# Products of the 64x64 inverse in four array tiles, with the second head's base written across the partition halves

## What is computed

```python
def wkv7_scan(r, w, k, v, kk, a, reverse):
    ...
    def step(state, inp):
        r_t, w_t, k_t, v_t, kk_t, a_t = inp
        sa = jnp.einsum('bhij,bhj->bhi', state, -kk_t)
        state = (state * w_t[:, :, None, :] + sa[..., None] * (kk_t * a_t)[:, :, None, :]
                 + v_t[..., None] * k_t[:, :, None, :])
        return state, jnp.einsum('bhij,bhj->bhi', state, r_t)
    ...
y = direction(0, False) + direction(1, True)
```

## Time and profile before

| | us |
|---|---|
| median of three runs | 3975.27 |
| lowest, highest | 3974.74, 3975.91 |
| the profiled execution | 3977.9 |
| its span, first to last instruction | 3976.1 |
| recurrence, layer 0 and layer 1 | 249.1 and 246.9 |

### The profile page before, as it was taken

How to read it: one execution, slowest core, us unless ns; L and a number is a source line. 1 busy time by engine, 2 the same in 40 slices (tenths; PEclk the granted TensorE clock), 3 DMA queues, 4 the chain that set the end, 5 groups by cost and what they waited for, 6 DMA issues and landing times.

```text
span 3976.1 us, 67100 instructions
## 1 busy us (share of the span) xinstructions
PE 3783.7 (95%) x28976; PEld 3059.2 (77%) x28976; DVE 1684.3 (42%) x2714; ACT 1439.1 (36%) x2442; POOL 1388.7 (35%) x581
## 2 busy tenths in 40 slices
PE   8888999999999889999999989999999999999999
PEld 7777778788887776688888776777888777787887
DVE  5554541577145554603682257414111376332112
ACT  3354252232323442523223243634222436424222
POOL 4001324434442002244444354133444443244443
PEclk9999999999999999999999999999999999999999
DMA  3001222276220002122473221112222221122222
GB/s 143 2 4 45 82 75 85 85 251 222 93 87 33 4 4 91 66 85 106 161 269 123 93 85 64 43 64 101 92 99 88 103 85 39 51 103 84 86 101 90
DMA packets 37150, 356.65 MB, mean 90 GB/s; under 512 B 4224, under 2 KB 4352, under 8 KB 17920
## 3 DMA queue, kind: packets, MB, share of 16 engines
q1 hardware_dynamic: 19584, 278.93, 18.9%
q10 hardware_dynamic: 17280, 73.48, 5.2%
HBM read 350.29 MB, written 2.10 MB: 89 GB/s over the span
## 4 chain that ended last, share of the span: by engine, by line
PE 84%; DVE 8%; ACT 3%; issue 2%; POOL 1%; DMA 1%; DVEq 0%; SPq 0%; PEldq 0%; ACTq 0%; PEld 0%; POOLq 0%
PE banks L757 23%; PE banks L759 23%; PE banks L758 22%; PE banks L1110 10%; PE banks L2151 3%; ACT arena L1471 1%; ACT arena L2304 1%; PE banks L2233 1%; POOL ring_r L855 1%; DMA ring<-stream 1%; DVE arena L1949 1%; DVE arena L2628 1%; PE banks L1217 0%; DVE arena L2627 0%; DVE arena L1843 0%
## 5 line engine op out<-in xcount | busy, mean ns | idle before, releaser
L855 POOL TENSOR_TENSOR ring_r<-ring,hi_ring 128x1024 fp32r<-128x1024 f32 x490 | 1202.4, 2458 | 2252.0 <-ACT hi_ring L846 2250.9
L757 PE MATMUL banks<-xT_r,ring_r 128*128 128x512 f32 (+1 forms) x2480 | 955.6, 385 | 25.8 <-issue 14.1
L759 PE MATMUL banks<-xT_r,hi_ring 128*128 128x512 f32 x2096 | 829.2, 396 | 0.0
L758 PE MATMUL banks<-x_lo_r,hi_ring 128*128 128x512 f32 x2096 | 825.4, 394 | 0.0
L846 ACT ACTIVATE hi_ring<-ring 128x1024 fp32r<-128x1024 f32 x490 | 511.3, 1047 | 734.0 <-DMA ring<-stream 289.2
L757 PEld LDWEIGHTS banks<-xT_r,ring_r 128*128 128x128 f32 x2480 | 472.5, 191 | 124.5 <-issue 26.7
L759 PEld LDWEIGHTS banks<-xT_r,hi_ring 128*128 128x128 f32 x2096 | 396.1, 189 | 94.1
L758 PEld LDWEIGHTS banks<-x_lo_r,hi_ring 128*128 128x128 f32 x2096 | 398.2, 190 | 90.3 <-issue 3.3
L1110 PE MATMUL banks<-arena 64*64 64x64 f32 (+4 forms) x7456 | 350.0, 246 | 53.0 <-DVE arena L1843 23.8
L1471 ACT ACTIVATE arena<-banks 128x512 f32<-128x512 f32 x366 | 214.7, 595 | 413.8 <-PE banks L759 255.2
L757 PE MATMUL banks<-hi_ring,pairs 128*128 128x512 f32 x864 | 341.8, 396 | 4.0 <-POOL ring_r L855 4.0
(11 more groups left out here) (263 smaller groups left out, 5504.1 us busy)
## 6 DMA issues: line engine op xcount, KB each, us to landing
ring<-stream SPq DMA_DIRECT2D x132, 2048.0 KB, 7.7
arena<-ada ACTq DMA_DIRECT2D x96, 512.0 KB, 4.9
arena<-ln_rows ACTq DMA_DIRECT2D x5, 1024.0 KB, 7.7
arena<-edge ACTq DMA_DIRECT2D x4, 1024.0 KB, 5.1
arena<-edge ACTq DMA_DIRECT2D x2, 1792.0 KB, 8.3
arena<-pack ACTq DMA_DIRECT2D x2, 1485.0 KB, 6.6
arena<-pack ACTq DMA_DIRECT2D x2, 1200.5 KB, 5.5
x<-x_in SPq DMA_DIRECT2D x4, 512.0 KB, 7.4
```

The lines of the kernel that those rows point to most:

```text
L757: first = nc.tensor.matmul(out_, left[1], right[0], start=start, stop=False)
L758: low = nc.tensor.matmul(out_, left[0], right[1], start=False, stop=False)
L759: return first, low, nc.tensor.matmul(out_, left[0], right[0], start=False, stop=stop)
L855: nc.gpsimd.tensor_tensor(feed.raw(n, ring_r), feed.raw(n), feed.hi(n).bitcast(F32), ALU.subtract).then_inc(split_lo, 1)
```

## The change

The operands keep their places except for head 1's part of `XT`, which now lies in the other partition half from the beginning. VectorE writes the base so: head 0 in one operation of 128 partitions, head 1 in two of 64 partitions, each into the opposite half. With this, x0, r0, inv_a and inv_x of all levels and wu run in four tiles, and inv_t of all levels in two, in bank 6. turned 0 becomes a product with the identity, in four tiles, that writes across the group's own two banks; it waits for gram 1's masks. turned 1 moves to bank 6. r0 moves from the beat of inv_a 4 to the beat of turned 2, into the group's own banks. wu's outputs are divided between its banks by head and no longer by chunk pair, so both banks are full at its end.

```diff
@@ -164,12 +164,12 @@
     b0, b1 = ((0, 1), (2, 3))[d]
     turned = [("v_rows", j, (6,))] if d == 0 else []
     out = [[("prep", g, (b0, b1))], [], [("prep_w", g, ())], [], [("prep_a", g, ())], [], [("prep_b", g, ()), ("prep_ar", g, ())],
-           [("gram", g, 0, (b0, b1))], [("gram", g, 1, (b0, b1)), ("unit", g, ())], [("turned", g, 0, (6,))] + turned,
-           [("x0", g, (b0,)), ("turned", g, 1, (b1,))], [("turned", g, 2, (6,))]]
+           [("gram", g, 0, (b0, b1))], [("gram", g, 1, (b0, b1)), ("unit", g, ())], [("turned", g, 0, (b0,))] + turned,
+           [("x0", g, (b0,)), ("turned", g, 1, (6,))], [("turned", g, 2, (6,)), ("r0", g, (b0,))]]
     for n in range(len(LEVELS)):
         last = n == len(LEVELS) - 1
-        banks_a, banks_x, banks_t = (b0,), (b0,) if n else (6,), (b0,) if n == 0 or last else (6,)
-        out += [[("inv_a", g, n, banks_a)] + ([("r0", g, (6,))] if last else []),
+        banks_a, banks_x, banks_t = (b0,), (b0,), (6,)
+        out += [[("inv_a", g, n, banks_a)],
                 ([] if last else [("inv_x", g, n, banks_x)]) + [("inv_t", g, n, banks_t)]]
     out += [[("wu", g, (b0, b1))], [("mq", g, (b0, b1))], [("oo", g, ())]]
     out += [[("link", g, i, (4 + i % 2,) if i < NC - 1 else ())] for i in range(NC)]
...
-        return name == "inv_t" and level in (0, len(LEVELS) - 1) or name in ("inv_a", "inv_x") and level > 0
+        return name in ("inv_a", "inv_x", "x0", "r0")
...
                 g, which = args
                 b = banks[0]
                 take(b, use[0])
-                for q in range(4):
-                    src = ARI[g % 3][:, 0, q * P:(q + 1) * P] if which == 0 else BB[g % 2][:, which - 1, q * P:(q + 1) * P]
-                    ins = nc.tensor.transpose(bank[b][:, q * P:(q + 1) * P], src, C("ident"))
+                if which == 0:
+                    drained(pe, uses, "gram", g, 1)
+                    for q in range(4):
+                        for e in range(2):
+                            for p_ in range(2):
+                                at = (4 * e + q) * CH
+                                ins = mm(across(b)[side(p_ ^ e), at:at + CH], ARI[g % 3][side(e), 0, (2 * q + p_) * CH:(2 * q + p_ + 1) * CH],
+                                         C("ident2")[side(e)], True, True)
+                else:
+                    drained(pe, uses, "turned", g, 0)
+                    for q in range(4):
+                        ins = nc.tensor.transpose(bank[b][:, q * P:(q + 1) * P], BB[g % 2][:, which - 1, q * P:(q + 1) * P], C("ident"))
                 ins.then_inc(bank_full[b], 1)
...
                 elif name == "r0":
                     drained(pe, uses, "gram", g, 1)
                     drained(pe, uses, "v_rows", g // 2)
+                    drained(pe, uses, "turned", g, 1)
                 elif name != "inv_a":
                     drained(pe, uses, "inv_a", g, args[1])
...
                             n, straight, crossed = 2 * q + e, side(p_), side(p_ ^ e)
-                            h = crossed if level and name in ("inv_x", "inv_t") else straight
-                            to = crossed if name == "inv_a" and level or name == "inv_t" and level < len(LEVELS) - 1 else straight
+                            h = straight if name in ("inv_a", "r0") else crossed
+                            to = straight if name in ("x0", "inv_x") else crossed
...
                 for q in range(4):
                     for e in range(2):
                         for p_ in range(2):
-                            h = side(p_)
-                            ins = mm(bank[banks[q // 2]][h, (q % 2 * 2 + e) * P:(q % 2 * 2 + e + 1) * P], XT[d][h, 2 * q + e, :],
+                            h = side(p_ ^ e)
+                            ins = mm(bank[banks[e]][side(p_), q * P:(q + 1) * P], XT[d][h, 2 * q + e, :],
                                      AR0[d][h, q, e, :, :].rearrange("p a t -> p (a t)"), True, True)
-                    if q % 2:
-                        ins.then_inc(bank_full[banks[q // 2]], 1)
+                        if q == 3:
+                            ins.then_inc(bank_full[banks[e]], 1)
...
-                out_ = AR0[d][:, :, :, 0, :] if which == 0 else GM[d][:, :, :, which - 1, 2, :]
-                f(out_, bank[b][:, :].rearrange("p (q e k) -> p q e k", q=4, e=2), ACT.Copy).then_inc(bank_free[b], 1)
-            elif name in ("inv_x", "inv_t") and wide(name, args[1]):
+                if which == 0:
+                    f(AR0[d][:, :, :, 0, :].rearrange("p q e k -> p e q k"), across(b).rearrange("p (e q k) -> p e q k", e=2, q=4), ACT.Copy)\
+                        .then_inc(bank_free[b], 1)
+                else:
+                    f(GM[d][:, :, :, which - 1, 2, :], bank[b][:, :].rearrange("p (q e k) -> p q e k", q=4, e=2), ACT.Copy)\
+                        .then_inc(bank_free[b], 1)
+            elif name in ("x0", "inv_x"):
...
                   across(b).rearrange("p (e q t) -> p e q t", e=2, q=4), ACT.Copy).then_inc(bank_free[b], 1)
-            elif name in ("x0", "inv_x", "inv_t"):
+            elif name == "inv_t":
...
-                f(AR0[args[0] % 2][:, :, :, 1, :], bank[b][:, :].rearrange("p (q e k) -> p q e k", q=4, e=2), ACT.Copy)\
+                f(AR0[args[0] % 2][:, :, :, 1, :].rearrange("p q e k -> p e q k"), across(b).rearrange("p (e q k) -> p e q k", e=2, q=4), ACT.Copy)\
                     .then_inc(bank_free[b], 1)
...
-                    f(WU[args[0] % 2][:, 2 * i:2 * i + 2, :, :, :].rearrange("p q e a t -> p (q e a t)"), bank[banks[i]][:, :], ACT.Copy)\
+                    f(WU[args[0] % 2][:, :, i, :, :].rearrange("p q a t -> p q (a t)"), bank[banks[i]][:, :].rearrange("p (q c) -> p q c", q=4), ACT.Copy)\
                         .then_inc(bank_free[banks[i]], 1)
...
                 low_t = GM[d][:, :, :, 0, 0, :].rearrange("p q e t -> p (q e) t")
                 up = C("first_L")[:, 64 * (1 - d):64 * (2 - d)]
                 link(V.tensor_tensor(low_t, low_t, C("ident2").unsqueeze(1).to_broadcast([P, 8, CH]), ALU.add))
-                V.tensor_tensor(XT[d], low_t, up.unsqueeze(1).to_broadcast([P, 8, CH]), ALU.mult).then_inc(first_done, 1)
+                by_head = [a.rearrange("p (q e) t -> p q e t", e=2) for a in (XT[d], low_t)]
+                V.tensor_tensor(by_head[0][:, :, 0, :], by_head[1][:, :, 0, :], up.unsqueeze(1).to_broadcast([P, 4, CH]), ALU.mult)
+                for h in range(2):
+                    ins = V.tensor_tensor(by_head[0][64 - 64 * h:128 - 64 * h, :, 1, :], by_head[1][64 * h:64 * h + 64, :, 1, :],
+                                          up[64 * h:64 * h + 64].unsqueeze(1).to_broadcast([CH, 4, CH]), ALU.mult)
+                ins.then_inc(first_done, 1)
```

## The result

The changed kernel takes **3998.62 us** (3990.03 to 4007.35, seven runs) where the kernel before, on the same chip, takes 3975.91 (3974.74 to 3983.31, seven runs): a ratio of 1.0052, 95% interval 1.0040 to 1.0063. It is slower by 0.5%, by 22.7 us. The forecast was 3962, its range ended at 3971, and slower had a chance of 0.05. The profiled execution took 4000.89 with a span of 3999.1, 23.0 more than before.

What follows compares the result with a forecast made beforehand. TensorE, busy in 95% of the span, was taken as the bound. Three even periods at 1.31 us, four odd at 0.69 and the ends gave 6.7 us a layer, 13.3 in two: 3975.3 became 3962 us, range 3951 to 3971.

Steps and rivals of the forecast that it cites:

- The pace of the products: TensorE in the recurrence: four tiles instead of two save 0.41 us per narrow product and 0.86 for wu.
- oo's pace: Feared for turned 0's 16 matmuls changing row halves: 1.05 us per 32 records against 0.51, costing 3 us in all.
- The base: VectorE before x0: three operations take 1.27 us instead of 0.69, 0.58 later, hidden under wu in even groups.
- The walk of a period: TensorE from gram 1 to oo in one group: gain of 0.44 us in even groups, loss of 0.18 in odd.
- From oo to the next gram 0: Later part of every period: inv_a 0 saves 0.41 us, and inv_a 1 starts 0.46 earlier through its new bank.
- The middle: Seven periods a layer between the ends: three even ones save 1.31 us each, four odd ones 0.69 each.
- Ends: First and last group of a layer: -1.0 against 0.87 us at the head, about +0.1 at the tail.
- rival (3): Added waits in the recurrence drop the clock to 1.2 GHz, two stretches per period, 45 us lost, 4007; chance 0.04.
- r0: Moved behind turned 2, where TensorE doesn't wait, it costs 0.51 us before oo in each group.
- (1): Rival: the recurrence's new waits are absorbed and nearly the bare sum of 26.9 us is saved, 3951; chance 0.10.
- (2): Rival: new waits eat more, each half-wide base operation taking 0.69 us, 3973; turned 0 possibly slow too; chance 0.18.
- (4): Rival: the recurrence's products stay at the two-tile pace because pairs meet in a bank, 3991; chance 0.02.

Runs made afterwards that it cites:

- a_base1: Changed kernel with VectorE's base as one 128x512 operation again (output not the reference's): 3998.6 us, ratio 1.0059.
- b_sh128: Kernel before with 32 tiny matmuls (128 TensorE instructions) added in the wait at the program's start: 3983.7 us, ratio 1.0007.
- a_fill: Changed kernel with products nobody reads in TensorE's waits, 32 at the head and 16 at the tail of each recurrence: 3985.6 us, ratio 1.0028.
- c_r0_head: Changed kernel with r0 at its old place in two tiles, output right, and products nobody reads at each head: 3968.4 us, ratio 0.9976.
- b_r0: Kernel before with r0 alone moved to the beat of turned 2, in two tiles as before: 3991.1 us, ratio 1.0043.
- a_r0old: Changed kernel with r0 back behind inv_a of level 4, in two tiles (output not the reference's): 3976.7 us, ratio 0.9999.
- a_sh64: Changed kernel with 16 tiny matmuls (64 TensorE instructions) added in the wait at the program's start: 3995.7 us, ratio 1.0037.
- c_r0: Changed kernel with r0 at its old place in two tiles, output right through two more ScalarE copies: 3974.5 us, ratio 0.9991.
- b_fill: Kernel before with products nobody reads in TensorE's waits at the head and tail of each recurrence: 3981.3 us, ratio 1.0021.
- a_w2: Changed kernel with eight products nobody reads in group 0 of each layer, before turned 0 and x0: 3983.3 us, ratio 1.0015.

## Why the prediction was wrong

**The pace of the products: right.** x0, r0, inv_a 0 and turned 0 at 0.69 to 0.73, wu at 1.10, as forecast from the earlier trace rows. turned 0 did not run at oo's pace.

**The base: its length right, its price too high.** Three operations from 278.71 to 280.00, 1.29 end to end where I took 1.27; VectorE's rows:

```profile
277.99 0.69 DVE L1849 TENSOR_TENSOR ring<-ring,const 128x512 f32<-128x512 f32 x1
278.71 0.42 DVE L1851 TENSOR_TENSOR arena<-ring,const 128x256 f32<-128x256 f32 x1
279.15 0.85 DVE L1853 TENSOR_TENSOR arena<-ring,const 64x256 f32<-64x256 f32 x2
```

0.42 + 0.85 and 0.02 between them: no overlap, where operations on the same partitions overlap by 0.09. The rule of the Trainium skill ("VectorE: DVE Perf Modes", section "Two Vector instructions with no wait between them") says that the crossing ones are held; the trace agrees. Against a_base1 the longer base delays x0 by 0.59 in the odd group, as forecast, but only 0.21 of it is left at the next gram 0, where my sum let all of it through.

**The walk of a period: misses that cancel, which is luck.** I let turned 0 and x0 start 0.1 before the last VectorE operation ends; they start 0.15 after it (280.00 to 280.15). So turned 0 comes at 5.17 after gram 0 and not at 4.94, and oo at 11.00 and 10.71 where the walk gave 10.62 and 10.44. So oo is 0.06 earlier in the even group and 0.45 later in the odd one, against 0.44 earlier and 0.18 later. From oo to the next gram 0 the forecast gave 0.87 and the trace gives 1.26 and 1.05. The sums, 1.32 and 0.60 a period against 1.31 and 0.69, agree only because of both.

**The middle: right without the stops.** Mean of after, its repeats and its shifts, against before and b_sh128: 437.2 - 24.4 = 412.8 against 434.3 - 10.8 = 423.5, 10.7 us less where the forecast's seven periods gave 13.4. (The few stops in heads and tails are taken off here too.)

**First failed step: a term that was not there.** The sum has no place for instruction supply. The stops grew by 13.6 us (24.4 against 10.8) and took the middle's gain. That they are waits for the instruction packet rests on the constant rest modulo 256 under two shifts, on one packet for every 256 instructions, and on the 2.15 us before which no boundary was crossed. Before, 4.4 us of "issue" stood among the waits of the same stretch; I did not ask what would make them more. The Trainium skill ("Runtime: NRT & Kernel Launch", section "Instruction fetch mechanics") says that the stream comes in blocks of 256 instructions and that crossing a boundary is mostly hidden. The block size agrees with the trace; hidden the crossing is here only where TensorE arrives 2.2 to 2.9 us after the packet's start or later. Four dense four-tile products are 256 instructions in about 2.05 us (a step of 0.51 each), four of two tiles take 3.7 (0.92 each): that is an estimate of why the shorter products stop and the longer ones seldom did. turned 0 adds 56 instructions a group.

**Second failed step: "Ends".** I put -1.0 + 0.87 on the head and +0.1 on the tail. At a clock of 1.00 the head of a_fill is 15.6 against 14.4 before, 1.2 longer where I had 0.13, so the head's term was mis-sized by about 1.1 a layer even without the clock (with r0 at its old place, c_r0_head, the head is 14.6). The clock came on top: 41.7 against 30.3 in the heads, 35.7 against 31.2 in the tails, 15.9 us in all by the same means. With these, 13.6 of stops and 2.7 missing in the middle the forecast's 3962 becomes 3994; the changed kernel's medians are 3992.5 to 4000.1. The low clock is the mechanism of rival (3). Its price held: the head of layer 0 stood at 0.50 for 13.7 us, four stretches of 3.4, and lost 5.0 against a_fill's, 1.3 each, where the earlier trace rows gave 1.4. Its place did not. I looked for it in the middle, two in each period, found nothing there that spoke for it, and wrote against it that the only one stood where nothing overlaps. There the change added waits: turned 0 for gram's masks (1.48), turned 2 for a copy (0.69), beside x0's for the base (0.87, before 1.09):

```profile
126.45 0.69 PE L1110 MATMUL banks<-const,arena 64*64 64x64 f32 x32 [1.48 <-DVE ring L1840]
...
128.60 1.13 PE L1110 MATMUL banks<-const,arena 64*64 64x64 f32 x32 [0.87 <-DVE arena L1853]
...
131.46 1.12 PE L1226 MATMUL banks<-const,arena 128*128 128x128 f32 x4 [0.69 <-ACT ring L1481]
```

In the ten heads of the changed kernel the clock falls at three places: in three 1.6 to 1.7 us after gram 0 began, in the wait for its masks, which the kernel before has as well; in three at 4.5 to 5.0, in turned 0's wait; in four at 6.9 to 7.1, in x0's. So the new waits are not all that lets it fall. What differs is what follows: before it came back after 3.4 us, in the changed kernel after 13.7 to 20.5, and r0's move alone (b_r0) has 10.2 in one head.

The middle has few such stretches, one or two in each of the five profiles of the changed kernel, 18 in all 14 profiles of it and of its variants, none in the four of the kernel before and its variants. They belong to the first failed step: each of the 18 begins 1.0 to 2.1 us after the end of a stop of 1.1 to 1.8 us. TensorE's weight loads at such a stop in after, and the windows ahead of the fall and in it:

```profile
1331.81 0.26 PEld L1110 LDWEIGHTS banks<-arena,ring 64*64 64x64 f32 x11 [1.47 <-issue]
...
1329.60:1333.00 3.40, 1.49 (x59) 1.22 (x55) 1.33 (x4) 1.12 (x3) 0.00 (x0) 1.00 0.00 0
1333.00:1336.50 3.50, 3.33 (x82) 3.36 (x86) 2.48 (x5) 1.05 (x2) 0.00 (x0) 0.51 0.02 5
```

The profiled execution of after has some twenty in its recurrences, twice what rival (3) named as the point from which the kernel is slower.

**r0: the term right, the consequence not.** 0.51 forecast, 0.52 measured before oo. That its place would also change the stops (24.4 with it, 13.6 in a_r0old) was not seen.

The other rivals: (1) did not happen; (2)'s base at 0.69 each did not, nor did it matter; (4) no.

What stays open: why the low clock sets in at the tails in half of the cases only (both tails of after follow a stop of over 1 us, but in a_sh64's second it falls without any); what starts an instruction packet (it starts some 50 to 295 instructions ahead of the boundary); how much of r0's 22 us is the stops' alignment, since c_r0_head has 20.6 us of them again and c_r0 14.8. No run takes the stops away and leaves the rest.

## What to carry to other kernels

Price a faster operation where nothing runs beside it, too: the first and last rounds of a pipelined loop are where shorter products leave TensorE thin, and there the clock can take back more than all rounds gave; a few products that nobody reads, in the waits, keep it, and where it would not have fallen they cost (7.7 us in b_fill). Before packing small products tighter, look at the waits on "issue": where they grow from a row in the profile into stops at a fixed rest of 256 instructions, as here, much of what shorter products save goes into waiting for their instructions. And move nothing out of a place where its engine waited anyway: r0's move cost more than four tiles gave it.

## What the runs showed that I had not expected

- TensorE stopped for 0.25 to 1.8 us here and there in dense 64x64 products: 10 us in two recurrences before, 20 to 27 in the changed kernel, always at 195 or 196 modulo 256 of its count; each such product is 64 instructions and takes 0.69 us at the 2.4 GHz level in four tiles.
- Once at 0.50, the clock stays there for 13.7 to 20.5 us in a head in which TensorE goes on working (15.1 busy us of 20.6), though the same head with eight more products in it (a_w2) does not fall at all, or for 3.4 us alone. In the middle of a recurrence it fell only behind a stop of over 1 us.
- The same program differs by several us in its middle and by 10 in its tails from execution to execution (31.1, 36.7 and 41.6 us in three profiles of the changed kernel), while the heads repeat within 0.1.
